# Upper weight parts of the expert stages made at mid-block instead of at block end

## The reference

```
t = h.reshape(b * length, d)                       # tokens x 2048
q = (t @ w_query)...                               # two half keys per head
... top 16 of 128 per half key, top 16 of 256 sums, gate = softmax(best)
u_sel = expert_u[ec]                               # 16384 experts in all
a = gelu(einsum('cd,chkd->chk', tc, u_sel))
w = gc * a
out = einsum('chk,chkd->cd', w, expert_v[ec])
```

## Time and profile before

| | us |
|---|---|
| time, median of 3 runs | 2011.15 (2009.04 to 2018.51) |
| profiled execution, its own time | 2014.42 |
| its span | 2012.6 |
| granted TensorE clock, mean | 0.995 of full speed |
| PE busy | 1959.7 (97% of the span) |
| PE weight loads busy | 1733.0 (86%) |
| DVE busy | 1660.5 (83%) |
| ACT busy | 1137.2 (57%) |
| POOL busy | 693.5 (34%) |

### The profile page before, as it was taken

The page is one execution under the profiler, slowest core; times in us unless marked ns, Lnnn a source line. Parts: engine busy times, 40 slices in busy tenths (PEclk is TensorE's granted clock), DMA queues, the critical chain, the costliest instruction groups (busy, mean ns, idle before and its releaser), DMA issues. The chain is left out here.

```text
span 2012.6 us, 32396 instructions
## 1 busy us (share of the span) xinstructions
PE 1959.7 (97%) x11584; PEld 1733.0 (86%) x11584; DVE 1660.5 (83%) x2375; ACT 1137.2 (57%) x1624; POOL 693.5 (34%) x372
## 2 busy tenths in 40 slices
PE   5999999999999999999999999999999999999988
PEld 4899899999978888999999999999777777777766
DVE  6666676667777767999999999999888888988877
ACT  5655566556577545656556565655455555555544
POOL 1011100111000000888888888886222221322220
PEclk9999999999999999999999999999999999999999
DMA  5556645565545555999998999999999999999996
GB/s 184 201 188 199 195 158 186 190 200 173 180 150 190 181 177 178 318 333 322 316 330 308 333 328 330 345 399 385 337 380 373 374 373 370 386 368 385 366 352 219
DMA packets 137298, 566.41 MB, mean 281 GB/s; under 512 B 43832, under 2 KB 51904, under 8 KB 87712
## 3 DMA queue, kind: packets, MB, share of 16 engines
q1 hardware_dynamic: 87456, 415.36, 57.4%
q0 software_dynamic: 49648, 148.44, 21.9%
q10 hardware_dynamic: 144, 2.10, 0.3%
HBM read 548.30 MB, written 16.88 MB: 281 GB/s over the span
## 5 line engine op out<-in xcount | busy, mean ns | idle before, releaser
L434 DVE TENSOR_TENSOR wlo<-raw,whi 128x1024 fp32r<-128x1024 f32 x242 | 295.2, 1229 | 150.8 <-PE psum L575 90.2
L764 PE MATMUL psum<-xr,whi 128*128 128x384 f32 x2048 | 380.8, 337 | 0.0
L787 PE MATMUL psum<-whi,xr 128*128 128x512 f32 x1524 | 368.9, 391 | 6.4 <-DVE xr L1556 6.0
L571 PE MATMUL psum<-xr,whi 128*128 128x512 f32 x1408 | 362.4, 399 | 8.7 <-DVE xr L1374 5.3
L764 PEld LDWEIGHTS psum<-xr,whi 128*128 128x128 f32 x2048 | 351.0, 188 | 0.4
L787 PEld LDWEIGHTS psum<-whi,xr 128*128 128x128 f32 x1524 | 286.7, 188 | 68.9 <-DVE xr L1556 7.1
L440 ACT ACTIVATE whi<-raw 128x2048 fp32r<-128x2048 f32 x169 | 322.7, 1909 | 26.0 <-DMA raw<-u_cols 13.2
L571 PEld LDWEIGHTS psum<-xr,whi 128*128 128x128 f32 x1408 | 253.4, 190 | 59.0 <-issue 6.2
L1166 POOL DMA_INDIRECT arena<-v_rows,small x64 | 143.5, 2242 | 407.5 <-DVE arena L1521 405.6
L427 ACT ACTIVATE whi<-raw 128x1024 fp32r<-128x1024 f32 x244 | 249.5, 1054 | 39.6 <-DMA raw<-stream 24.5
L1166 POOL DMA_INDIRECT arena<-u_rows,small x64 | 103.2, 1612 | 331.3 <-DMA small<-arena 308.3
(11 more groups left out here) (265 smaller groups left out, 3125.2 us busy)
## 6 DMA issues: line engine op xcount, KB each, us to landing
raw<-stream SPq DMA_DIRECT2D x244, 512.0 KB, 3.4
raw<-v_rows SPq DMA_DIRECT2D x85, 1024.0 KB, 7.8
raw<-u_cols SPq DMA_DIRECT2D x84, 1024.0 KB, 6.7
arena<-v_rows SPq DMA_DIRECT2D x43, 1024.0 KB
arena<-u_cols SPq DMA_DIRECT2D x42, 1024.0 KB
gates<-arena POOLq DMA_DIRECT2D x8, 1536.0 KB, 9.6
small<-gates SPq DMA_DIRECT2D x62, 192.0 KB, 8.4
arena<-x_t SPq DMA_DIRECT2D x4, 544.0 KB, 6.5
```

Of the source, the lines that this page charges most:

```text
L434: nc.vector.tensor_tensor(wlo[:, k % 2 * HALF:(k % 2 + 1) * HALF], raw[:, s * HALF:(s + 1) * HALF], f(whi[:, s * HALF:(s + 1) * HALF]), AL ...
L571: mm(bank(b), whi[:, s * HALF + c * P:s * HALF + (c + 1) * P], both[c], start=start and c == 0, stop=False)
L764: mm(bank(at, 0, 2 * TD), hi_w[:, c * P:(c + 1) * P], z_all[:, :, c, 0:TD // TS, :], start=c == 0, stop=False)
L787: last = mm(at[:, (b * 4 + j * 2 + n) * 512:(b * 4 + j * 2 + n + 1) * 512], weights, src, start=begin, stop=end, skip_group_check=True)
```

## The change

PE counts a new semaphore (`hi_used`) when the last matmul with the upper part of a block has ended. ACT makes the upper part of block n+2 once that count and the lower part of block n are there, ahead of its wait for the end of block n. So in ACT's order L440 stands ahead of the copy L1091 (U stage) and ahead of the rounding L1080, L1081 (V stage), where it stood behind them.

```diff
                 pe.wait_ge(hi_done, base * 2 + 2 * b + 2)
                 for c in range(KC):
-                    mm(bank(at, 0, 2 * TD), hi_w[:, c * P:(c + 1) * P], z_all[:, :, c, 0:TD // TS, :], start=c == 0, stop=False)
+                    last = mm(bank(at, 0, 2 * TD), hi_w[:, c * P:(c + 1) * P], z_all[:, :, c, 0:TD // TS, :], start=c == 0,
+                              stop=False)
+                last.then_inc(hi_used, 1)
                 pe.wait_ge(lo_done, base * 2 + 2 * b + 1)
...
-                        part(1, j, psum, Wboth[q], False, first, False)
+                        last = part(1, j, psum, Wboth[q], False, first, False)
...
+                last.then_inc(hi_used, 1)
                 pe.wait_ge(lo_done, base * 2 + 2 * F_V + 2 * c + 2)
...
+            def upper_parts(n):
+                act.wait_ge(hi_used, n + 1)
+                act.wait_ge(lo_done, 2 * F_U + 2 * n + 2)
+                hi_block(act, n + 2)
+
             for n in range(B_U):
                 if n == B_U - 1:
                     weight_hi(0, 0)
+                upper_parts(n)
                 act.wait_ge(half_done, 2 * F_U + 2 * n + 2)
...
                 A(one_weight(n), bank(U_BANKS[n % 4], TD, TD), ACT.Copy).then_inc(low_part, 1)
-                hi_block(act, n + 2)
                 if n:
                     gelu(n - 1)
...
             for c in range(B_V - 2):
+                upper_parts(B_U + c)
                 act.wait_ge(half_done, 2 * F_V + 2 * c + 2)
                 weight_hi(c + 2, c % 2)
-                hi_block(act, B_U + c + 2)
```

More of the change, by code:

```diff
@@ L377, in hybrid_layer @@
         hi_done, lo_done, half_done = sem("hi_done"), sem("lo_done"), sem("half_multiplied")
-        bank_free = sem("bank_free")
+        bank_free, hi_used = sem("bank_free"), sem("upper_parts_multiplied")
         low_copied, low_added = sem("x_lo_half_copied"), sem("x_lo_half_added")
@@ L810, in value_block @@
                     pe.wait_ge(low_residual, residual + 1)
-                    part(1, residual, psum, Wboth[q], False, False, False)
+                    last = part(1, residual, psum, Wboth[q], False, False, False)
+                last.then_inc(hi_used, 1)
                 pe.wait_ge(lo_done, base * 2 + 2 * F_V + 2 * c + 2)
```

## The result

The changed kernel takes 2036.96 us (median of 4 runs, 2031.8 to 2038.14) against 2012.49 before (4 runs, 2009.04 to 2018.51), a ratio of 1.0115 (95% interval 1.0097 to 1.0134). It is 24 us slower, and 2033 us was forecast. The profiled execution has a span of 2036.2 us, 23.6 more than before.

A forecast was written before the change was run, and what follows sets the result against it. PE, DVE and DMA engines were all taken as at their limit in the U stage, PE in the V stage. 19 + 2.5 + 2 - 2 = 21.5 us on the median 2011.15 gave 2033 us, range 2012 to 2055.

The forecast's parts named there:

- The U stage: U stage: late tiles delay the copy, DVE's sum and PE, +19 us; earlier upper parts win back 2 us.
- The number of late tiles: U stage: ACT waits for a tile landing after the copy's old place 19 times in 107 blocks.
- the case given nothing: U stage: tile lands between mid-block and the copy's old place, copy up to 2.1 us late; bounds 0 and 10 us.
- The idle time on VectorE: U stage: each late tile leaves DVE idle 1.65 us beyond its margin, 38 us in the stage.
- half of it reaches PE: U stage: of DVE's 38 us idle time half is taken to delay PE, +19 us; bounds 0 and 38.
- the reasons it gave for halving: U stage: late places between two PE waits count once, the larger; longer blocks give transfers more time; small delays pass on nothing.
- The gain: U stage: L440 starts about 2 us earlier, saving DVE's 2.7 us wait for upper parts; 2 us counted.
- From U to V: Last U block: L440 goes before the copy, so the sum and PE's first V block come later, +2.5 us once.
- The V stage: V stage: rounding waits behind L440; average late tile just covered, latest 0.4 us too late; +2 us, bounds 0 and +7.
- The prediction's rule of the Trainium skill: V stage: weight loads' busy share measures headroom, up to 130 us by the rule; the prediction kept 0.

The follow-up runs named there:

- The four-slot pair: Old and new order with one gathered-row buffer made a fourth U-stage tile slot, tiles loaded one block earlier, against the kernel before: 2024.4 and 2020.68 us.
- the count alone: Kernel before plus PE's count of the new semaphore; ScalarE does not wait for it and keeps the old order: 2013.51 us against 2015.52.
- the kernel with the U stage alone: New order on ScalarE only in the U stage, V stage as before, against the kernel before: 2035.01 us against 2015.52, ratio 1.0093.

## Why the prediction was right

**The U stage.** Forecast +19 less 2, measured +24.2 between the first and the last upper-part matmul. The mechanism was right: a late tile, then the copy, then VectorE, then PE, and without the copy the loss is gone. The number of late tiles was right too. Forecast were 19 in 107 blocks, 23 in the stage; block by block, 24 tiles of the changed kernel held L440 beyond its old place, 0.43 us after the block's end. The 60 waits shown above are more because the wait now starts at mid-block: 48 further tiles of the stage landed between mid-block and there. They were the case given nothing, and they made VectorE wait 4.1 us.

Two other terms were mis-sized, and their errors have opposite signs. The idle time on VectorE was put at 38 us, 1.65 in each late place; all its waits for the copy in the stage come to this:

```profile
DVE arena L1569 <- ACT arena L1100: 32.6, 24, 3.7
```

Before it was 2.5 us in 5 times, so the change added 30.1; the 24 late places have 27.6 of the 32.6, and ten of them cost VectorE nothing. And "half of it reaches PE" was far too low: the stage is 24.2 us longer and VectorE's idle time grew by 24.7, so nearly all of it reached the length of the stage. That fits what the prediction had read first, that VectorE is what PE waits for; the reasons it gave for halving were not borne out. That the total came so near is in part luck: half of too much.

**The gain.** It was put at 2 us from the one row in which VectorE waits for upper parts. A second row, shown above, has 1.5 more; over the stage such waits were 4.4 us, and in the changed kernel there are none. So the gain was real, twice as large as forecast, and a seventh of what the copy cost. The four-slot pair hints at the same, with the new order 3.7 us below the old one by the medians, but the intervals overlap.

**From U to V.** The wait was forecast at 2.5 us more and measured at 2.55 (2.95 against 0.40). What was left out is what followed: while the clock was down the block took 2.9 us more. The Trainium skill (TensorE: Matmul & The Clock Gate, Part 1) says that the slow clock is the default and that activity lifts it. The trace agrees in this: the granted clock is 0.89 in the 2 us in which PE does nothing, 0.50 over the next 6, 0.90 in the 2 after that, and then 1.00; PE is at work in all of these but the first. That the slow clock is the default no run here shows.

**The V stage.** Forecast +2; alone its new order changes nothing, 1.0000. VectorE's spare time covered the late tiles, as the bound of 0 had it, though L440 now waited for a tile up to 4.3 us from 1500 to 1900 us. The prediction's rule of the Trainium skill (Perfetto Trace Analysis, Identifying the Most-Contended Engine), by which weight loads at 77.5 of 100 us would be headroom, was not put to the test: in this stage PE hardly ever waited for an upper part, so an earlier one had nothing to give it.

**The baseline's stop.** The profile of before has one V block 8 us too long, from 1938 to 1951 us: PE waits 5.06 us in it and then runs at a granted clock of about 0.5 for 6 us. It is not the new order's to win: the same block is 1.4 us too long with the count alone, 5.7 with the last U block in the old order, 8.3 in the old order with four slots. It differs between executions, and the profile of the kernel before happens to hold one of the long ones. In the comparison of the two profiles it stands against the 5.4 us of the first V block and a few short stops of the changed kernel, so the V stage looks 1.1 us longer; that near balance is no sign that the V stage took the change as costed.

## What to carry to other kernels

On an engine that works in order, where an instruction may stand is a question about everything behind it: ask how long it will wait at its new place when its input comes late, and price even the smallest instruction behind it by who needs that. Here a copy of 0.33 us decided, not the pass of 1.91 us that was moved. Doing something earlier pays only where its input is there earlier too and somebody waits for the result: here 72 of 127 tiles of the U stage came after mid-block, and the waits that it could save were 4.4 us. And where an engine has only 3% of idle time left, as VectorE had here, idle time added to it has to be counted nearly in full.

## What had not been expected of the hardware

A wait of 2.95 us on PE cost 5.4 us, since the granted clock stood at 0.50 for about 6 us after it; a wait of 1.66 us at the same place in the kernel with the U stage alone left ten matmuls at 2.56 us, full speed. But the length of the wait alone does not decide it. In the changed kernel's U stage PE waited 1.71 us and the clock stayed, and 1.58 us and it fell:

```profile
832.63 2.03 PE L771 MATMUL psum<-xr,wlo 128*128 128x192 f32 x16 [1.71 <-DVE wlo L450]
939.11 2.36 PE L771 MATMUL psum<-xr,wlo 128*128 128x192 f32 x16 [1.58 <-DVE wlo L450]
```

The stretch behind each (columns as above):

```profile
834.00:838.00 4.00, 4.00 (x29) 4.00 (x29) 3.84 (x11) 1.70 (x4) 3.39 (x3) 1.00 0.85 270
942.00:944.00 2.00, 2.00 (x8) 2.00 (x7) 2.00 (x3) 1.34 (x3) 1.89 (x1) 0.50 1.00 422
```

Halving the bytes of the weight tiles made the old order only 6 us faster and its U stage no shorter, with the DMA engines 0.96 and 0.97 busy before: a share near one did not mean that the kernel waited for its transfers.
